# Context part of a gated delta kernel: silu ahead of a weight chunk's split, row sums from a repeated rate column

## The chip, the cores and the metric

One Trainium2 chip, one of its NeuronCores. The metric is device time in microseconds of one execution. Engines: PE (TensorE) multiplies, DVE (VectorE), ACT (ScalarE) and POOL (GpSimd) work elementwise, SP issues the weight loads.

## The reference, cut to what matters

Two model blocks over 256 positions of width 1024: a first block of two layers (attention, pooling, a feed-forward part of width 4096, a gate), and a second block whose mixer runs a chunked gated delta rule over a context and then over the latent positions. The change touches the inputs of that rule:

```python
qkv = jax.nn.silu(conv_fn(p_qkv, conv_w))        # then q, k, v; k is l2-normalized
g = -jnp.exp(a_log) * jax.nn.softplus(alpha + dt_bias)
g = jnp.cumsum(g, axis=-1)                       # per chunk, head and direction
decay = jnp.exp(jnp.where(lower, g[..., :, None] - g[..., None, :], -jnp.inf))
a = jnp.where(strict, jnp.einsum("bhnid,bhnjd->bhnij", kb, k) * decay, 0.0)
```

The kernel takes chunks of 128, two of them, four heads, two directions: four groups g = 0 to 3 of [128, 4 x 128]. The decay needs the cumulative sum of g once down the partitions and once along the row, the same row in all partitions: the row sums.

## The kernel before, in words

All values are fp32. A weight matrix comes in chunks of 1 MB from SP's queue into a ring of four raw slots. For the large projections each chunk is split in two halves into a high part (ACT, `split_hi`, line 534) and a low part (DVE, `split_lo`, line 543), in a ring of four pieces, and PE makes three products for each tile (lines 552 to 554). PE frees a piece when it has used it; a raw slot is free when its low parts are made.

The engines run programs in written order and meet at semaphores. PE's results go to eight PSUM banks. `Banks.claim` makes PE wait until all earlier uses of a bank are freed by their readers. In layer 1 the projections, the context's convolution inputs and the whole context delta part take banks 4 to 7 in turn (`ring([4, 5, 6, 7])`), in this order of claims: six query and key projections, `u`, three value projections, the context's rates, `ctx_c0` to `ctx_c3`, `out0`, two sums of squares `l20` and `l21`, `cum`, `out1`, `out2`, `kt0`, `vt0`, `kt1`, `vt1`, `out3`, and then the row sums `grow` and products `kk` with feed-forward steps between.

The context's delta part (`pe_delta`, `act_delta`, `dve_delta`, `pool_delta`, called with "ctx") runs in layer 1 between steps of the layer's own output projection and feed-forward part: `fill(point)` runs the next step, at all engines at the same point. Step `out0` (chunk 10) is at the point "ba", `out1` and `out2` (chunks 11 and 12) at "norm", `out3` at "tok", `up0` and on at "T0", "T1" ... The same functions run once more for the latent part.

Ahead of the delta part: the last convolution of the context's keys and values (ACT's middle line 749, DVE's sides lines 758 and 763); then ACT splits chunk 11 and makes the silu of keys and values in one instruction (line 1954), loads the table of logarithm and exponential (line 548), and begins `act_delta` with the exponentials and the logarithm of the rates (lines 988 to 991). DVE makes the low split of chunk 11, then the rates (lines 1114 to 1122), the squares of the keys (line 1132), the finished rates (lines 1136 to 1140, `dn_g`), and in the step of `out0` adds its bank to `h` (line 2467), which frees the bank. PE runs `out0`, sums the squares over the partitions with a matrix of ones (line 818), makes the cumulative sums (lines 825, 826), then `out1`. POOL waits for `dn_g`, makes four products of the triangular mask (`cum0` or `cum1`) with the rate columns of four heads (line 1297, `dn_tg`), then two copies of identity parts (line 1301). PE's row sum of a group is one matmul of ones with such a product (line 844).

Of the kernel before, what the change touches and what calls it, by code (L numbers as in the profile page):

```python
# [23 lines left out]
ALU = mybir.AluOpType  # L24
ACT = mybir.ActivationFunctionType
AX = mybir.AxisListType

P = 128
# [13 lines left out]
DN_H = 4  # L42
# [105 lines left out]
def vec_columns():  # L148
# [5 lines left out]
    for name, n in TILE_B:  # L154
# [25 lines left out]
LAST_FILL = 6 + len(LAT_FILL)  # L180


CTX_TOLD = dict(ba=1, ba2=1, sq=2, kn=2, rs=2, g=1, gcol=1, ecol=1, bcol=1, tok=1, tg=4,
                dl=4, el=4, A=4, P=2, T=2, XI=2, X=2 * LEVELS, Z=2 * (LEVELS - 1), N=2 * (LEVELS - 1), T2=2 * (LEVELS - 2),
                vb=4, kd=4, uw=4, vnew=2, state=4)

# [66 lines left out]
CTX_LAYER = 1  # L253
# [79 lines left out]
def two_blocks(nc, a, out):  # L333
    K, NK = const_columns()
    V, ROWS_A, NV = vec_columns()
    with ExitStack() as ctx:
# [5 lines left out]
        def S(name):  # L342
            if name not in sems:
                sems[name] = ctx.enter_context(nc.semaphore(name))
            return sems[name]
# [29 lines left out]
        ps = [ctx.enter_context(nc.psum_tensor(f"bank{b}", [P, 512], F32)) for b in range(8)]  # L375
# [23 lines left out]
        def col(name, i=0, n=1):  # L399
            s = K[name][0] + i  # L400
            return kt[:, s:s + n]
# [17 lines left out]
        g_X = A(4, 512)  # L419
# [96 lines left out]
        def chunk(layer, s):  # L516

            if s < LAYER_CHUNKS:
                return layer, s
            return (layer + 1, s - LAYER_CHUNKS) if layer + 1 < DEPTH else ("post", s - LAYER_CHUNKS)  # L520

        def split_hi(act, name, halves=(0, 1)):

            n = st.width(name)
            for half in halves:
                slot = st.piece(name, half)
                if name == (0, 0) and half == 0:
                    act.wait_ge(S("first_half"), 16)
                elif name == (0, 0) or half == 0:
                    act.wait_ge(landed[st.slot(name)], st.loads(name))  # L530
                v = st.pieces(name, half) - PIECES
                if v > 0:
                    act.wait_ge(pieces_done, v)
                nc.scalar.activation(whi[:, slot, 0:n], raw[:, st.slot(name), n * half:n * (half + 1)],  # L534
                                     ACT.Copy).then_inc(hi_ready, 1)
# [10 lines left out]
        def ln_exp_tables():  # L546

            nc.scalar.preload_act_table_set("natural_log_exp_and_others")
# [115 lines left out]
        def per_head(v):  # L664

            return v.unsqueeze(2).broadcast_to([P, DN_H, P])

        def all_heads(v):
            return v.unsqueeze(1).broadcast_to([P, DN_H, v.shape[1]])

        def h4(v):
            return v.rearrange("p (h n) -> p h n", h=DN_H)
# [5 lines left out]
        def chunk_of(g):  # L678
            return g // 2, g % 2
# [126 lines left out]
        def pe_delta(pe, part, d_, take, fill):  # L806
# [3 lines left out]
            F = banks.filled  # L810
# [18 lines left out]
            for n in range(TT):  # L829
                pe.wait_ge(*told("kn", 2))  # L830
                b = C(f"kt{n}")
                for hh in range(DN_H):
                    mm = nc.tensor.transpose(ps[b][:, P * hh:P * (hh + 1)], k_n[:, hh, P * n:P * (n + 1)], ident)
                F(mm, b)
                b = C(f"vt{n}")
                for hh in range(DN_H):
                    mm = nc.tensor.transpose(ps[b][:, P * hh:P * (hh + 1)], v_n[:, hh, P * n:P * (n + 1)], ident)
                F(mm, b)
            fill("tok")
            for i, g in enumerate(BY_CHUNK):  # L840
                d, n = chunk_of(g)
                pe.wait_ge(*told("tg", g + 1))
                b = C(f"grow{g}")
                F(nc.tensor.matmul(ps[b][:, :], ones, g_X[:, g, :], start=True, stop=True), b)
                if d == 0:
                    b = C(f"kk{g}")
                    for hh in range(DN_H):
                        kk = k_n[:, hh, P * n:P * (n + 1)]
                        mm = nc.tensor.matmul(ps[b][:, P * hh:P * (hh + 1)], kk, kk, start=True, stop=True)
                    F(mm, b)  # L850
                if lat and d == 0:
                    b = C(f"qk{g}")
                    if g == 0:
                        pe.wait_ge(S("lat_qn"), 2)
                    for hh in range(DN_H):
                        mm = nc.tensor.matmul(ps[b][:, P * hh:P * (hh + 1)], k_n[:, hh, P * n:P * (n + 1)],
                                              q_n[:, hh, P * n:P * (n + 1)], start=True, stop=True)
                    F(mm, b)
                fill(f"T{i}")
# [115 lines left out]
        def act_delta(act, part, d_, fill, settle=None):  # L975
# [13 lines left out]
            nc.scalar.activation(ba_t2, ba_t2, ACT.Exp, scale=-1.0)  # L989
            act.drain()  # L990
            nc.scalar.activation(ba_t2, ba_t2, ACT.Ln, bias=1.0).then_inc(S("dn_ba2"), 1)

            fill("ba")
            for i in range(4 if lat else 2):
# [102 lines left out]
        def dve_delta(dve, part, d_, fill):  # L1097
# [26 lines left out]

            nq = 4 if lat else 2
            first = 0 if lat else 4
            dve.wait_ge(S("silu"), 1 + len(lat_tiles) if lat else 1)
            for i in range(nq):
                v = sil[:, first + 2 * i:first + 2 * i + 2, :]
                if i >= 2:  # L1130
# [8 lines left out]
            nc.vector.reciprocal(ba_beta, ba_t1)  # L1139
            nc.vector.tensor_tensor(ba_g, ba_g, two(neg_a[:, :]), ALU.mult)  # L1140
            dve.drain().then_inc(S("dn_g"), 1)
            fill("ba")
            for i in range(nq):
                v = sil[:, first + 2 * i:first + 2 * i + 2, :]
# [143 lines left out]
        def pool_delta(pool, part, d_):  # L1288
            lat = part == "lat"
            told = lambda name, n: (S("dn_" + name), n + (CTX_TOLD[name] if lat else 0))  # L1290
            g_v = nc.gpsimd
            g_A, g_X, g_T = d_.A, d_.X, d_.T
            pool.wait_ge(*told("g", 1))
            for g in range(4):
                d, n = chunk_of(g)

                g_v.tensor_tensor(h4(g_X[:, g, :]), all_heads(col(f"cum{d}", 0, P)),
                                  per_head(d_.ba_g[:, n, 4 * d:4 * d + 4]), ALU.mult).then_inc(S("dn_tg"), 1)

            for n in range(TT):  # L1300
                g_v.tensor_copy(d_.rest(g_T, n), per_pair(ident))
            for n in range(TT if lat else 0):
                pool.wait_ge(*told("A", 2 * n + 2))
                g_v.tensor_tensor(g_A[:, n, :], g_A[:, n, :], g_A[:, 2 + n, :], ALU.add)
                pool.drain()
                g_v.tensor_tensor(h4(g_A[:, 2 + n, :]), h4(g_A[:, n, :]), all_heads(col("sib", 0, P)), ALU.mult)
                pool.drain().then_inc(S("dn_P"), 1)
                g_v.tensor_tensor(d_.other(g_T, n), per_pair(ident),
                                  g_A[:, 2 + n, :].rearrange("p (h n s) -> p h n s", h=DN_H, s=2), ALU.subtract)
                pool.drain().then_inc(S("dn_T"), 1)  # L1310
            if not lat:
                pool.drain().then_inc(S("ctx_rest"), 1)
                return
            pool.wait_ge(*told("ecol", 1))
            pool.wait_ge(*told("tok", 1))
            pool.wait_ge(S("lat_qn"), 2)
            for g in range(4):
                d, n = chunk_of(g)
                pool.wait_ge(S("lat_egrow"), BY_CHUNK.index(g) + 1)
                g_v.tensor_tensor(h4(g_q[:, g, :]), tok(d_.q, n), h4(g_q[:, g, :]), ALU.mult).then_inc(  # L1320
                    S("lat_qg"), 1)
            pool.wait_ge(S("lat_attn"), 4)
            pool.drain()
            for g in range(4):
                d, n = chunk_of(g)
                g_v.tensor_tensor(h4(d_.kd[:, g, :]), d_.ktok[:, n], per_head(d_.kd_col[:, g, :]), ALU.mult).then_inc(
                    S("dn_kd"), 1)
            pool.wait_ge(*told("bcol", 1))
            for g in range(4):
                d, n = chunk_of(g)  # L1330
                if g >= 2:
                    pool.wait_ge(*told("uw", g - 1))
                g_v.tensor_tensor(h4(d_.vb[:, g % 2, :]), d_.vtok[:, n], per_head(d_.beta_of(g)), ALU.mult)
                g_v.tensor_tensor(h4(d_.kb[:, g % 2, :]), d_.ktok[:, n], per_head(d_.bg_col[:, g, :]), ALU.mult)
                pool.drain().then_inc(S("dn_vb"), 1)
# [423 lines left out]
        def _(act):  # L1759
# [43 lines left out]
            for layer in range(DEPTH):  # L1803
# [122 lines left out]
                for kind, x in ATT[layer]:  # L1926
# [19 lines left out]
                    elif kind == "conv":  # L1946
                        act.wait_ge(direct_done, st.direct["ctx", x] + 1)
                        b = banks.bank(f"ctx_c{x}")
                        conv_middle(D_CTX.sil, b, 4 + 2 * x).then_inc(S("conv1"), 1)
                split_hi(act, chunk(layer, 11))  # L1950
                if layer == CTX_LAYER:
                    act.wait_ge(S("conv"), 4)
                    kv = D_CTX.sil[:, 4:12, :]
                    nc.scalar.activation(kv, kv, ACT.Silu).then_inc(S("silu"), 1)
                    ln_exp_tables()

                todo = list(range(10, 46))

# [228 lines left out]
        def _(dve):  # L2187
# [92 lines left out]
            for layer in range(DEPTH):  # L2280
# [166 lines left out]
                        free(ins, b)  # L2447
                    dve.drain().then_inc(S("cat_act"), 1)
                dve.drain().then_inc(S("side_free"), 1)
                split_lo(dve, chunk(layer, 11))  # L2450

                todo = list(range(10, 46))

# [403 lines left out]
```

## Time and profile before

| | us |
|---|---|
| median of 3 runs | 1300.92 (1298.52 to 1301.8) |
| the profiled execution's own time | 1299.26 |
| its span in the profile | 1297.5 |
| PE busy | 1248.8 |
| DVE busy | 872.7 |
| ACT busy | 640.3 |
| POOL busy | 93.5 |

An engine's busy time counts its instructions, not its waits. A matmul of unsplit fp32 operands leaves two records, and records of PE overlap, so times on PE are read from start to start. A row of a timeline merges consecutive instructions of one kind (xN); the bracket holds the idle time of the engine ahead of it and what ended it.

### The profile page before, as it was taken

To read this page: it belongs to the slowest core of one execution; us is meant where nothing else is said; L and a number is where in the kernel's file an instruction comes from. 1 tells how busy PE (TensorE), PEld (TensorE's weight loads), DVE (VectorE), ACT (ScalarE), POOL (GpSimd) and SP (SyncE) were. 2 spreads that over 40 slices of the span, in tenths; PEclk is the share of its full clock that TensorE was granted. 3 is DMA by queue.
4 is the path that set the end of the run, shared out by engine and by line. 5 is a ranking of instruction groups with operands and counts; after the bars stand their busy time and mean duration, and the time that the engine had idled before them with its cause. 6 is when DMAs were issued, how large, how long until landed. Compare 5 with 4: busy or idle time off the path is not lost.

```text
span 1297.5 us, 20646 instructions
## 1 busy us (share of the span) xinstructions
PE 1248.8 (96%) x8322; PEld 1107.1 (85%) x8322; DVE 872.7 (67%) x1312; ACT 640.3 (49%) x974; POOL 93.5 (7%) x84
## 2 busy tenths in 40 slices
PE   7989999999999998999999999999899999999997
PEld 7979778888998887899999889986789988888886
DVE  6886656667778478765646776785467776766665
ACT  6574434335656364545364665552254555444443
POOL 0330000000024020000000000324100000000000
PEclk9999999999999999999999999999999999999999
DMA  9634776555663453544543665537115556555530
GB/s 329 196 100 163 265 256 225 194 179 189 224 210 100 133 160 98 163 131 134 175 142 105 197 191 145 181 98 250 43 53 175 194 183 235 199 194 195 189 136 33
DMA packets 164620, 219.35 MB, mean 169 GB/s; under 512 B 5456, under 2 KB 135342, under 8 KB 164398
## 3 DMA queue, kind: packets, MB, share of 16 engines
q1 hardware_dynamic: 162800, 214.45, 50.9%
q10 hardware_dynamic: 1726, 3.59, 0.7%
q8 instruction: 66, 1.08, 0.4%
q14 instruction: 28, 0.23, 0.1%
HBM read 216.19 MB, written 1.05 MB: 167 GB/s over the span
## 4 chain that ended last, share of the span: by engine, by line
PE 75%; DVE 12%; ACT 4%; DVEq 3%; issue 2%; DMA 2%; SPq 1%; ACTq 1%
PE bank L552 14%; PE bank L596 14%; PE bank L554 13%; PE bank L553 13%; PE bank L598 7%; DVE w_lo L543 4%; PE bank L642 2%; DMA arena<-arena 2%; PE bank L886 1%; PE bank L874 1%; ACT w_hi L534 1%; PE bank L1438 1%; PE bank L1417 1%; SPq L2811 1%; PE bank L903 1%
## 5 line engine op out<-in xcount | busy, mean ns | idle before, releaser
L543 DVE TENSOR_TENSOR w_lo<-w_raw,w_hi 128x1024 fp32r<-128x1024 f32 (+1 forms) x350 | 418.0, 1239 | 86.1 <-ACT w_hi L534 78.4
L534 ACT ACTIVATE w_hi<-w_raw 128x1024 fp32r<-128x1024 f32 (+1 forms) x350 | 347.0, 1039 | 93.0 <-PE bank L554 58.1
L596 PE MATMUL bank<-act_parts,w_hi 128*128 128x512 f32 x800 | 283.7, 398 | 2.8 <-DVE act_parts L2206 1.4
L552 PE MATMUL bank<-act_parts,w_hi 128*128 128x256 f32 x944 | 272.1, 288 | 10.3 <-DVE w_lo L543 5.2
L554 PE MATMUL bank<-act_parts,w_lo 128*128 128x256 f32 x944 | 267.7, 284 | 0.0
L553 PE MATMUL bank<-act_parts,w_hi 128*128 128x256 f32 x944 | 267.7, 284 | 0.0
L598 PE MATMUL bank<-act_parts,w_lo 128*128 128x256 f32 x800 | 224.0, 280 | 0.0
L552 PEld LDWEIGHTS bank<-act_parts,w_hi 128*128 128x128 f32 x944 | 181.6, 192 | 19.0 <-issue 13.5
L596 PEld LDWEIGHTS bank<-act_parts,w_hi 128*128 128x128 f32 x800 | 150.1, 188 | 45.0 <-issue 7.2
L553 PEld LDWEIGHTS bank<-act_parts,w_hi 128*128 128x128 f32 x944 | 181.7, 193 | 0.5 <-issue 0.5
L554 PEld LDWEIGHTS bank<-act_parts,w_lo 128*128 128x128 f32 x944 | 181.6, 192 | 0.0
L552 PE MATMUL bank<-w_hi,side_hi 128*128 128x512 f32 (+1 forms) x392 | 150.1, 383 | 1.5 <-DVE w_lo L543 1.5
L598 PEld LDWEIGHTS bank<-act_parts,w_lo 128*128 128x128 f32 x800 | 151.0, 189 | 0.3
L554 PE MATMUL bank<-w_hi,side_lo 128*128 128x512 f32 (+1 forms) x392 | 148.0, 378 | 0.0
L553 PE MATMUL bank<-w_lo,side_hi 128*128 128x512 f32 (+1 forms) x392 | 147.7, 377 | 0.0
L608 DVE TENSOR_REDUCE arena<-bank 128x256 f32<-128x512 f32 x100 | 64.4, 686 | 84.9 <-PE bank L598 84.9
L552 PEld LDWEIGHTS bank<-w_hi,side_hi 128*128 128x128 f32 x392 | 73.8, 188 | 20.0 <-issue 6.8
L554 PEld LDWEIGHTS bank<-w_hi,side_lo 128*128 128x128 f32 x392 | 73.7, 188 | 14.0
L553 PEld LDWEIGHTS bank<-w_lo,side_hi 128*128 128x128 f32 x392 | 73.8, 188 | 12.3
L1980 ACT ACTIVATE side_hi<-arena 128x512 fp32r<-128x512 f32 x32 | 20.2, 632 | 118.6 <-DVE arena L2483 103.4
L552 PE MATMUL bank<-side_hi,w_hi 128*128 128x256 f32 x208 | 60.4, 291 | 4.5 <-DVE w_lo L543 4.5
L553 PE MATMUL bank<-side_lo,w_hi 128*128 128x256 f32 x208 | 59.6, 287 | 0.0
(333 smaller groups left out, 1606.4 us busy)
## 6 DMA issues: line engine op xcount, KB each, us to landing
w_raw<-in_w_in SPq DMA_DIRECT2D x39, 1024.0 KB, 6.0
w_raw<-in_w_up SPq DMA_DIRECT2D x32, 1024.0 KB, 5.6
w_raw<-in_w_down SPq DMA_DIRECT2D x32, 1024.0 KB, 5.0
w_raw<-in_w_mod SPq DMA_DIRECT2D x24, 1024.0 KB, 5.4
w_raw<-in_w_ffn_in SPq DMA_DIRECT2D x22, 1024.0 KB, 5.2
w_raw<-in_w_gate SPq DMA_DIRECT2D x20, 1024.0 KB, 5.1
w_raw<-in_w_ffn_out SPq DMA_DIRECT2D x11, 1024.0 KB, 5.4
w_raw<-in_w_out SPq DMA_DIRECT2D x8, 1024.0 KB, 5.1
```

The costliest lines, as they stand in the source:

```text
L534: nc.scalar.activation(whi[:, slot, 0:n], raw[:, st.slot(name), n * half:n * (half + 1)], ACT.Copy).then_inc(hi_ready, 1)
L543: nc.vector.tensor_tensor(wlo[:, slot, 0:n], raw[:, st.slot(name), n * half:n * (half + 1)], whi[:, slot, 0:n].bitcast(F32), ALU.subtract) ...
L552: nc.tensor.matmul(o, ahi, bhi, start=start, stop=False, skip_group_check=True)
L553: nc.tensor.matmul(o, ahi, blo, start=False, stop=False, skip_group_check=True)
L554: return nc.tensor.matmul(o, alo, bhi, start=False, stop=stop, skip_group_check=True)
L596: nc.tensor.matmul(pair(two_banks[m]), whi[:, slot, at:at + P], xall[:, :, f, :], start=f == 0, stop=False, skip_group_check=True)
L598: mm = nc.tensor.matmul(o[:, 0:T], wlo[:, slot, at:at + P], xhi[:, f, :], start=False, stop=f == KT - 1, skip_group_check=True)
L608: return nc.vector.tensor_reduce(to, ps[b][:, :].rearrange("p (s t) -> p t s", s=2), AX.X, ALU.add)
L642: mm = nc.tensor.matmul(ps[bank][:, T * m:T * (m + 1)], raw[:, st.slot(name), at:at + P], act[:, k, :], start=k == 0, stop=k == KT - 1)
L874: mm = nc.tensor.matmul(ps[b][:, P * hh:P * (hh + 1)], h4(g_A[:, n, :])[:, hh, :], d_.x_new_of(n, hh, lv), start=True, stop=True)
L886: mm = nc.tensor.matmul(ps[b][:, P * hh:P * (hh + 1)], h4(z_sm[:, n, :])[:, hh, :], d_.t_new_of(n, hh, lv), start=True, stop=True)
L1980: nc.scalar.activation(yhi[:, 2 * (j % 2):2 * (j % 2) + 2, :], relu2[j % 2], ACT.Copy).then_inc(S("relu_hi"), 1)
```

## The change

For the context, the split of chunk 11 moves from ahead of the silu (ACT) and ahead of the rates (DVE) to behind the rates' logarithm (ACT) and behind the finished rates (DVE), in both cases still ahead of the step of `out0`. The silu of keys and values becomes two instructions, keys first; DVE's squares wait for the first alone, PE's transposes of values for the second. Layer 0 keeps its order. In both parts, context and latent, POOL's four products are gone; each row sum is four matmuls, one for each head, whose weights are the head's rate column repeated in 128 columns and whose moving operand is the mask itself.

```diff
--- before.py
+++ after.py
@@ -180,7 +180,7 @@
 LAST_FILL = 6 + len(LAT_FILL)
 
 
-CTX_TOLD = dict(ba=1, ba2=1, sq=2, kn=2, rs=2, g=1, gcol=1, ecol=1, bcol=1, tok=1, tg=4,
+CTX_TOLD = dict(ba=1, ba2=1, sq=2, kn=2, rs=2, g=1, gcol=1, ecol=1, bcol=1, tok=1,
                 dl=4, el=4, A=4, P=2, T=2, XI=2, X=2 * LEVELS, Z=2 * (LEVELS - 1), N=2 * (LEVELS - 1), T2=2 * (LEVELS - 2),
                 vb=4, kd=4, uw=4, vnew=2, state=4)
 
@@ -833,15 +833,19 @@
                     mm = nc.tensor.transpose(ps[b][:, P * hh:P * (hh + 1)], k_n[:, hh, P * n:P * (n + 1)], ident)
                 F(mm, b)
                 b = C(f"vt{n}")
+                if not lat:
+                    pe.wait_ge(S("silu"), 2)
                 for hh in range(DN_H):
                     mm = nc.tensor.transpose(ps[b][:, P * hh:P * (hh + 1)], v_n[:, hh, P * n:P * (n + 1)], ident)
                 F(mm, b)
             fill("tok")
             for i, g in enumerate(BY_CHUNK):
                 d, n = chunk_of(g)
-                pe.wait_ge(*told("tg", g + 1))
                 b = C(f"grow{g}")
-                F(nc.tensor.matmul(ps[b][:, :], ones, g_X[:, g, :], start=True, stop=True), b)
+                for hh in range(DN_H):
+                    rate = d_.ba_g[:, n, 4 * d + hh:4 * d + hh + 1].broadcast_to([P, P])
+                    mm = nc.tensor.matmul(ps[b][:, P * hh:P * (hh + 1)], rate, col(f"cum{d}", 0, P), start=True, stop=True)
+                F(mm, b)
                 if d == 0:
                     b = C(f"kk{g}")
                     for hh in range(DN_H):
@@ -989,6 +993,8 @@
             nc.scalar.activation(ba_t2, ba_t2, ACT.Exp, scale=-1.0)
             act.drain()
             nc.scalar.activation(ba_t2, ba_t2, ACT.Ln, bias=1.0).then_inc(S("dn_ba2"), 1)
+            if not lat:
+                split_hi(act, chunk(CTX_LAYER, 11))
 
             fill("ba")
             for i in range(4 if lat else 2):
@@ -1124,7 +1130,7 @@
 
             nq = 4 if lat else 2
             first = 0 if lat else 4
-            dve.wait_ge(S("silu"), 1 + len(lat_tiles) if lat else 1)
+            dve.wait_ge(S("silu"), 2 + len(lat_tiles) if lat else 1)
             for i in range(nq):
                 v = sil[:, first + 2 * i:first + 2 * i + 2, :]
                 if i >= 2:
@@ -1139,6 +1145,8 @@
             nc.vector.reciprocal(ba_beta, ba_t1)
             nc.vector.tensor_tensor(ba_g, ba_g, two(neg_a[:, :]), ALU.mult)
             dve.drain().then_inc(S("dn_g"), 1)
+            if not lat:
+                split_lo(dve, chunk(CTX_LAYER, 11))
             fill("ba")
             for i in range(nq):
                 v = sil[:, first + 2 * i:first + 2 * i + 2, :]
@@ -1291,12 +1299,6 @@
             g_v = nc.gpsimd
             g_A, g_X, g_T = d_.A, d_.X, d_.T
             pool.wait_ge(*told("g", 1))
-            for g in range(4):
-                d, n = chunk_of(g)
-
-                g_v.tensor_tensor(h4(g_X[:, g, :]), all_heads(col(f"cum{d}", 0, P)),
-                                  per_head(d_.ba_g[:, n, 4 * d:4 * d + 4]), ALU.mult).then_inc(S("dn_tg"), 1)
-
             for n in range(TT):
                 g_v.tensor_copy(d_.rest(g_T, n), per_pair(ident))
             for n in range(TT if lat else 0):
@@ -1947,12 +1949,14 @@
                         act.wait_ge(direct_done, st.direct["ctx", x] + 1)
                         b = banks.bank(f"ctx_c{x}")
                         conv_middle(D_CTX.sil, b, 4 + 2 * x).then_inc(S("conv1"), 1)
-                split_hi(act, chunk(layer, 11))
                 if layer == CTX_LAYER:
-                    act.wait_ge(S("conv"), 4)
-                    kv = D_CTX.sil[:, 4:12, :]
-                    nc.scalar.activation(kv, kv, ACT.Silu).then_inc(S("silu"), 1)
+                    for half in range(2):
+                        act.wait_ge(S("conv"), 2 * half + 2)
+                        part = D_CTX.sil[:, 4 + 4 * half:8 + 4 * half, :]
+                        nc.scalar.activation(part, part, ACT.Silu).then_inc(S("silu"), 1)
                     ln_exp_tables()
+                else:
+                    split_hi(act, chunk(layer, 11))
 
                 todo = list(range(10, 46))
 
@@ -2447,7 +2451,8 @@
                         free(ins, b)
                     dve.drain().then_inc(S("cat_act"), 1)
                 dve.drain().then_inc(S("side_free"), 1)
-                split_lo(dve, chunk(layer, 11))
+                if layer != CTX_LAYER:
+                    split_lo(dve, chunk(layer, 11))
 
                 todo = list(range(10, 46))
```

## Rows read from the trace of the kernel before

**Rows 1.** The page's part 1: busy time, share of the span, instructions.
```profile
PE 1248.8 (96%) x8322; PEld 1107.1 (85%) x8322; DVE 872.7 (67%) x1312; ACT 640.3 (49%) x974; POOL 93.5 (7%) x84
```

**Rows 2.** Chain of waits, 453 to 466 us: start us, us, what.
```profile
460.98 0.70 DVE arena L1132
461.73 1.98 PE bank L818 x4
```

**Rows 3.** Timeline of PE, 459 to 468: start, us, operation, [idle before, releaser].
```profile
459.97 0.28 PE L554 MATMUL bank<-act_parts,w_lo 128*128 128x256 f32 x1
461.73 1.98 PE L818 MATMUL bank<-arena,consts_sb 128*128 128x512 f32 x4 [1.48 <-DVE arena L1132]
463.55 0.28 PE L825 MATMUL bank<-arena,consts_sb 128*128 128x4 f32 x2
465.25 0.36 PE L552 MATMUL bank<-act_parts,w_hi 128*128 128x256 f32 x1
```

**Rows 4.** Timeline of DVE there.
```profile
457.37 2.36 DVE L543 TENSOR_TENSOR w_lo<-w_raw,w_hi 128x1024 fp32r<-128x1024 f32 x2 [0.23 <-ACT w_hi L534]
459.65 0.22 DVE L1114 TENSOR_REDUCE arena<-bank 128x16 f32<-128x64 f32 x1
463.08 0.69 DVE L2467 TENSOR_TENSOR h<-h,bank 128x512 f32<-128x512 f32 x1
466.57 4.01 DVE L543 TENSOR_TENSOR w_lo<-w_raw,w_hi 128x1024 fp32r<-128x1024 f32 x2
```

**Rows 5.** Timeline of ACT there.
```profile
454.45 0.83 ACT L749 ACTIVATE arena<-bank,vec_cols 128x256 f32<-128x256 f32 x2
455.16 2.01 ACT L534 ACTIVATE w_hi<-w_raw 128x1024 fp32r<-128x1024 f32 x2
458.49 1.92 ACT L1954 ACTIVATE arena<-arena 128x2048 f32<-128x2048 f32 x1
460.42 1.28 ACT L548 ACT_TABLE_LOAD   x1
462.23 1.99 ACT L534 ACTIVATE w_hi<-w_raw 128x1024 fp32r<-128x1024 f32 x2
```

**Rows 6.** Timeline of PE, behind the fourth context row sums.
```profile
511.31 0.35 PE L552 MATMUL bank<-act_parts,w_hi 128*128 128x256 f32 x1 [3.45 <-DVE w_lo L543]
```

**Rows 7.** Timeline of PE, the transposes of values.
```profile
478.18 0.66 PE L837 MATMUL bank<-consts_sb,arena 128*128 128x128 f32 x4 [0.73 <-DVE arena L1153]
```

**Rows 8.** Timeline of POOL: context products and copies, latent products.
```profile
463.07 4.49 POOL L1297 TENSOR_TENSOR arena<-consts_sb,arena 128x512 f32<-128x512 f32 x4 [50.07 <-DVEq L1141]
467.50 4.08 POOL L1301 COPY arena<-consts_sb 128x512 f32<-128x512 f32 x2
...
815.70 6.46 POOL L1297 TENSOR_TENSOR arena<-consts_sb,arena 128x512 f32<-128x512 f32 x4 [344.12 <-DVEq L1141]
```

**Rows 9.** Timeline of SP and of ACT: a load's issue, its first reader.
```profile
459.76 0.37 SPq L2795 DMA_DIRECT2D w_raw<-in_w_up  x1
...
490.16 1.04 ACT L534 ACTIVATE w_hi<-w_raw 128x1024 fp32r<-128x1024 f32 x1
```

**Rows 10.** Chain of waits: row sums, key products; line 844's weight loads.
```profile
842.83 0.86 PE bank L844 x2
843.69 0.89 PE bank L849 x8
...
L844 PEld LDWEIGHTS bank<-arena,consts_sb x16: 188/191/192, 485.4 to 866.1; 128*128 128x128 f32 x16
```

**Rows 11.** What PE waited for, 796 to 880: total us, times, longest.
```profile
PE bank L866 <- POOLq L1307: 1.2, 1, 1.2
PE bank L552 <- DVE w_lo L543: 1.0, 1, 1.0
```

**Rows 12.** Stretches: window, length, busy of PE, PEld, DVE, ACT, POOL, PEclk, DMA.
```profile
461.70:465.20 3.50, 3.47 (x20) 2.52 (x20) 1.79 (x6) 3.33 (x8) 2.13 (x3) 1.00 0.81 265
511.98:515.36 3.38, 3.38 (x19) 3.38 (x17) 2.51 (x7) 1.63 (x3) 0.00 (x0) 0.50 0.53 131
```

## The prediction

> **What bounds the kernel now.** I read the page first: TensorE is busy 96% of the span, DVE 67%, ACT 49%, POOL 7% [rows 1]. So an edit on DVE, ACT or POOL is worth only the TensorE idle time that it removes or makes. Then the chain of waits around the place of the edit, and the timelines of the engines there.
>
> The chain shows how the context stage starts. TensorE finishes `out0` (last record from 459.97), has nothing, and starts the sums of squares at 461.73: 1.48 us idle, released by the DVE square of line 1132 [rows 2, 3]. On DVE that square stands behind the low split of weight chunk 11 (457.37 to 459.73) and the small rate operations (from 459.65) [rows 2, 4]. On ACT the high split of chunk 11 (455.16 to 457.17) stands ahead of the table load, the silu of keys and values, the second table load and the rates' exponentials [rows 5]. The edit takes both splits out of the way. The later stalls of this stage (3.45 us before 511.31, behind a low split) hang on DVE work that starts from `out3`, hence from TensorE, and move along with it [rows 6].
>
> **ACT and DVE, as they will run.** ACT, from the end of the last conv middle (454.45 + 0.83 = 455.28): table load 1.28, silu of keys, silu of values. The two halves have 128x1024 elements each. The trace has no silu of that size; the whole took 1.92, and a pair of 128x1024 copies 2.01, so I take 2.0 for the pair and 1.06 for the first. The second half waits for conv 4, which DVE ends at 457.14, before the first half ends at 457.6. So silu 1 is up at 457.65, silu 2 at 458.6, the second table load ends at 459.9, where it ended at 461.70: everything behind it is 1.8 us earlier [rows 5]. DVE has the rates from 457.3 instead of 459.65, ends them after the same 1.33 (460.98 minus 459.65), and squares at 458.6 and 459.2; the first square is written by 459.3. TensorE is then still in `out0`, so its 1.48 us are gone, and counted from record to record (461.73 minus 459.97 + 0.12) 1.6 us. The rates' logarithm comes 1.8 earlier, the finished rates at 463.05 - 1.8 = 461.25. TensorE wants them when the sums of squares are issued (1.82 after their start in the trace, so 462.0): no wait. The eight pairs of cumulative sums take 463.55 to 465.25, 1.70; they end at 463.7 [rows 3].
>
> **What is late next.** After them comes `out1`. It needs chunk 11, whose splits now stand behind the rates. ACT: 1.8 earlier than the split at 462.23, so 460.4 to 462.4 [rows 5]. DVE: from 461.5, and `out1` could read the first half at 462.7 to 463.5. That is early enough. But `out1` also claims a bank. The part takes banks 4 to 7 in turn; in the order of claims `out0` is number 16, the two sums of squares 17 and 18, the cumulative sums 19, `out1` number 20. So `out1` has the bank of `out0`, and waits until DVE has added `out0` to `h` (line 2467). I trust this count because it says the same of the transposes of values: they would have the bank of the cumulative sums, and the trace shows just that wait, 0.73 us on the copy of line 1153 [rows 7]. Before, the residual ran at 463.08 to 463.77, straight after the rates, and TensorE came at 465.25: 1.5 us of slack. Now the split of chunk 11 stands between the rates and the residual on DVE.
>
> How long is that split? Alone the two halves take 2.36 (457.37), while POOL works 4.01 (466.57) [rows 4]. POOL no longer makes its four products, 4.49 us; its two copies, 4.08 us, follow the rates at once, at 461.25 to 465.3, where they ran from 467.50 [rows 8]. In the trace these very copies lay beside the low split of chunk 12 and made it 4.01. So the removed products don't free DVE here, they bring the copies forward onto chunk 11. The low end is 2.36: the split ends at 463.9, the residual (0.69) at 464.55, and `out1` starts 0.7 earlier than before. The high end is 4.01: split to 465.5, residual to 466.1, `out1` at 466.15, against 465.25: 0.9 later. I take the high end, because both engines and both operations are the same as they were at 466.57 [rows 4, 8].
>
> The Trainium skill (SBUF — State Buffer, "SBUF: two separate sides") says that of a VectorE operation with two inputs in SBUF and a GpSimd operation that reads SBUF the one that starts second waits for the whole of the first. Estimated by that rule, with 1.12 for a copy alone (a quarter of POOL's four products), the split would start at 462.4, wait once more between its halves, and end at 465.9 instead of 465.5, and `out1` start 1.3 later instead of 0.9. The trace agrees that they collide (4.01 against 2.36), and the durations from it stand in my sum.
>
> TensorE is then idle from 463.7 to 466.15, some 2.4 us in place of 1.48. Behind it: the normalized keys (ACT's reciprocal root at about 465.6, 0.1 later than before) follow the residual on DVE at 466.1, the split of chunk 12 follows without POOL beside it (2.36, to 469.2), and `out2` wants it after 5.8 us of `out1`, at 471.9: no further wait. SP's load that needs chunk 11 split is issued some 5.7 us later than at 459.76; its data is first read at 490.16, by ACT: hidden [rows 9]. The load behind it needs chunk 12's split, which ends at 469.2 instead of 470.6. The transposes of values wait for silu 2, long there.
>
> **Row sums.** Each of eight becomes four fp32 matmuls of 128 columns in place of one of 512. Of the new kind the nearest is the keys' product: 8 records 0.89, the old 2 records 0.86: +0.03 each, 0.24 for eight [rows 10]. The weights are one column repeated, whose load I bound from both sides: nothing more than a full tile (0.89), or its load (191 ns) eight times in a row, 1.52, +0.66 each. I take the first, since the keys' products have eight such loads too and don't show them. Of the eight, those of the context lie ahead of the 3.45 us stall, which swallows them. Of the latent ones I count 0.1 in all. The latent part's POOL products (6.46 us) go too; nobody waited for them: between 796 and 880 TensorE waits 1.2 on POOL's parts after the decays and 1.0 on a weight split, neither of them behind the products [rows 8, 11]. DVE gets faster beside a shorter POOL there, at no gain on TensorE: 0.
>
> **Sum.** -1.6 for the stall, +2.5 for the new wait on the bank (net +0.9 at `out1`), +0.1 for the row sums: +1.0 us. The profiled execution took 1299.26 (span 1297.5 and 1.76 around it), so 1300.3; the median of the runs shown lies 1.66 above that execution, so 1301.9 against 1300.92. A change below 0.3%, 3.9 us, can't be told from none here.
>
> **Rivals.**
> (a) The copies and the split don't collide, or POOL's copies are through sooner: the low end above, -0.7 + 0.1 = -0.6, so 1300.3. For it: spans on POOL are rough, and the first copy starts a moment before the split. Against it: both copies together last longer than a lone split.
> (b) No wait on the bank at all: the full -1.6 + 0.1, 1299.4. Against it stand the count and the wait in [rows 7].
> (c) Slower: the longer idle time drops the clock. After the 3.45 us stall the trace shows TensorE at 0.50 of its clock (1.2 GHz) for 3.38 us, so 1.7 us of work lost; after the 1.48 us stall it stays at 1.00 [rows 3, 6, 12]. The new gap of 2.4 lies between. There the loss was covered by DVE; in `out1` nothing covers it: +1.0 + 1.7 = +2.7, 1303.6. It decides if a gap of 2.4 us is already enough, and it costs all that was won at the sums of squares, and more. The Trainium skill (TensorE: Matmul & The Clock Gate, "The HAM clock gate") says that idleness throttles the engine to half clock; by it this case is possible and not sure.
> (d) Slower: the repeated column is dear, the high end above. Context mostly covered by the stall, latent four at +0.66, and two of the context that the stall does not cover: +4.0 on top of +0.9, 1305.8.
>
> **How the numbers follow.** Forecast 0.50, (a) 0.17, (b) 0.08, (c) 0.18, (d) 0.03, other 0.04. The runs shown differ by 3.3 us among themselves, so a median is uncertain by more than these cases differ. Range 1298.0 to 1305.0. Faster by over 0.3% (below 1297.0) would take (b) and luck: 0.03; slower by over 0.3% (above 1304.8) takes (d), or (c) and bad luck: 0.05; within: 0.92.
>
> **What would show it.** In the profile after: the sums of squares start within 0.2 us of `out0`'s end; then a TensorE idle of 2 to 2.6 us before `out1`, released by line 2467's residual; the low split of chunk 11 just ahead of that at about 2 us a half, with POOL's copies beside it from 461.3; no POOL products. Halves at 1.2 mean (a); no idle ahead of `out1` means that the bank count is wrong, (b); half clock in `out1` means (c); row sums of more than 0.9 us mean (d).

## The result, and the profile after

| | before | after |
|---|---|---|
| median | 1300.59 us (1298.28 to 1302.26, 20 runs) | 1302.57 us (1300.61 to 1305.89, 20 runs) |
| ratio | | 1.0021, 95% interval 1.0014 to 1.0027 |
| profiled execution's span | 1297.5 | 1302.3 |

The changed kernel is 0.2% slower, 2.7 us by the ratio. That is inside the range and below the 0.3% that were set as a bound, but its interval is clear of 1. The likeliest case had +1.0; +2.7 is what rival (c), half clock in `out1`, was priced at.

The page's part 1 of the changed kernel, against [rows 1]: TensorE works 2.9 us longer, POOL 12.5 less.

```profile
PE 1251.7 (96%) x8370; PEld 1113.9 (86%) x8370; DVE 869.0 (67%) x1312; ACT 640.3 (49%) x975; POOL 81.0 (6%) x76
```

The timeline of TensorE at the same place, against [rows 3]. `out0`'s end to the sums of squares: no idle any more. The cumulative sums end at 463.7; then TensorE idles 2.16 us, and what ends it is line 2472, DVE's residual of `out0`:

```profile
460.20 1.88 PE L818 MATMUL bank<-arena,consts_sb 128*128 128x512 f32 x4
461.91 0.28 PE L825 MATMUL bank<-arena,consts_sb 128*128 128x4 f32 x2
465.92 0.58 PE L552 MATMUL bank<-act_parts,w_hi 128*128 128x256 f32 x1 [2.16 <-DVE h L2472]
```

The timeline of DVE, against [rows 4]. The rates come first, then the squares; the low split of chunk 11 takes 3.66 us in place of 2.36, and the residual waits behind it. Chunk 12's split, 4.01 before, takes 2.35:

```profile
457.47 0.23 DVE L1120 TENSOR_REDUCE arena<-bank 128x16 f32<-128x64 f32 x1 [0.23 <-issue]
458.81 1.29 DVE L1138 TENSOR_TENSOR arena<-arena 128x512 f32<-128x512 f32 x2
461.61 3.66 DVE L543 TENSOR_TENSOR w_lo<-w_raw,w_hi 128x1024 fp32r<-128x1024 f32 x2 [0.34 <-ACT w_hi L534]
465.19 0.67 DVE L2472 TENSOR_TENSOR h<-h,bank 128x512 f32<-128x512 f32 x1
466.61 2.35 DVE L543 TENSOR_TENSOR w_lo<-w_raw,w_hi 128x1024 fp32r<-128x1024 f32 x2
```

ACT, against [rows 5]: the two halves of the silu (x2, 2.01), the table load, and one run of four high splits (chunks 11 and 12). POOL, against [rows 8]: only the copies are left, beside chunk 11's low split, in 3.00 us where they took 4.08.

```profile
455.40 1.28 ACT L1956 ACT_TABLE_LOAD   x1
456.70 2.01 ACT L1956 ACTIVATE arena<-arena 128x1024 f32<-128x1024 f32 x2
458.72 1.28 ACT L548 ACT_TABLE_LOAD   x1
460.53 3.88 ACT L534 ACTIVATE w_hi<-w_raw 128x1024 fp32r<-128x1024 f32 x4
```

```profile
461.36 3.00 POOL L1303 COPY arena<-consts_sb 128x512 f32<-128x512 f32 x2 [48.26 <-DVEq L1147]
```

Four stretches of the changed kernel, with columns as in [rows 12] (window, length, busy of PE, PEld, DVE, ACT, POOL, granted clock, DMA). In the 7 us from the start of `out1` TensorE is busy all the time at a mean clock of 0.57: 3.0 us of work lost. Ahead of the gap it had 1.00, and the clock fell inside the gap: it is 1.00 up to 464.76 and 0.50 from 465.26 on. After the first stall of the stage, 3.35 us long, it stays at 1.00 (514.65 to 519.90). It has half clock once more, for about 3.4 us, after the second stall:

```profile
458.00:464.00 6.00, 5.76 (x40) 4.71 (x38) 4.76 (x12) 5.90 (x9) 2.64 (x2) 1.00 0.01 1
465.92:472.92 7.00, 7.00 (x36) 7.00 (x37) 2.96 (x3) 1.06 (x1) 0.00 (x0) 0.57 0.86 281
514.65:519.90 5.25, 5.25 (x44) 5.25 (x45) 4.17 (x9) 2.53 (x3) 0.00 (x0) 1.00 0.58 161
523.20:526.20 3.00, 3.00 (x7) 2.43 (x8) 2.30 (x4) 1.38 (x2) 0.00 (x0) 0.50 0.32 33
```

The two stalls of DVE's stretch in the changed kernel; [rows 6] has the first of them:

```profile
514.65 0.36 PE L552 MATMUL bank<-act_parts,w_hi 128*128 128x256 f32 x1 [3.35 <-DVE w_lo L543]
523.20 0.77 PE L552 MATMUL bank<-w_hi,side_hi 128*128 128x512 f32 x1 [2.56 <-DVE w_lo L543]
```

Starts of the same matmuls in both traces show where the 4.8 us of the two profiled executions come from: `out1` 465.25 and 465.92 (+0.67); first matmul after the stall of 3.4 us, 511.31 and 514.65 (+3.34); second stall 519.91 and 523.20 (+3.29); the first matmul of the step after that, 526.59 and 531.12 (+4.53); the last transposes 1290.02 and 1294.95 (+4.93). So +0.7 is the wait, +2.7 the half clock in `out1`, and +1.2 the second half clock, behind the second stall; the last 0.4 arises later in the kernel, and its cause is open. The trace before has half clock in this stage only after the first stall (from 511.98), where DVE is the bound. Where half clock falls behind the two stalls is a matter of the single execution, and so is the +1.2: the medians differ by 2.0.

A row sum and a product of keys in the latent part, in the chain of waits, against [rows 10]: 0.89 each.

```profile
847.32 0.89 PE bank L847 x8
848.21 0.89 PE bank L853 x8
```

### The profile page after: what moved, and what is told of

The parts are those of the page before. It is cut to its first block, busy times and chain, and to the rows that moved or that the text cites. A ratio compares the mean times of both kernels' runs of the same rounds, so it can differ in the third digit from the quotient of the medians.

```text
span 1302.3 us, 20729 instructions
## 1 busy us (share of the span) xinstructions
PE 1251.7 (96%) x8370; PEld 1113.9 (86%) x8370; DVE 869.0 (67%) x1312; ACT 640.3 (49%) x975; POOL 81.0 (6%) x76
## 4 chain that ended last, share of the span: by engine, by line
PE 77%; DVE 11%; ACT 5%; DVEq 3%; issue 2%; DMA 2%; ACTq 1%; SPq 0%
PE bank L552 14%; PE bank L554 14%; PE bank L553 14%; PE bank L596 14%; PE bank L598 7%; DVE w_lo L543 4%; PE bank L642 2%; PE bank L890 1%; PE bank L1419 1%; PE bank L878 1%; PE bank L1440 1%; DMA arena<-arena 1%; ACT w_hi L534 1%; PE bank L907 1%; DVE arena L1239 1%
## 5 line engine op out<-in xcount | busy, mean ns | idle before, releaser
L554 PE MATMUL bank<-side_hi,w_lo 128*128 128x256 f32 x208 | 59.6, 286 | 0.0
```

The lines of the kernel that those rows point to most:

```text
L554: return nc.tensor.matmul(o, alo, bhi, start=False, stop=stop, skip_group_check=True)
```

## The experiments

All ratios are against the kernel before, on the same chip, 95% interval in brackets. Executions differ by up to 3.3 us in when they reach this place, so `out1` is told from the start of the last convolution middle on ACT (line 749), which lies ahead of all that is changed. In the trace before that distance is 465.25 - 454.45 = 10.80 us. "Clock" is the mean granted clock in the 7 us from the start of `out1`. "At the stall" measures from the same ACT instruction to the first matmul after the stage's first stall, the one at 511.31 in the trace before (distance 56.86), and gives the difference to before: what a kernel has lost or won when `out1` and the steps behind it are done. Gap, distances and clock come from the one profiled execution of each kernel, the ratio from all its executions.

| kernel | gap before `out1` | distance | against before | clock | at the stall | ratio |
|---|---|---|---|---|---|---|
| before | none | 10.80 | | 1.00 | | |
| changed | 2.16 | 11.37 | +0.57 | 0.57 | +3.24 | 1.0021 (1.0014 to 1.0027) |
| e1 matmuls in the gap | 0.17 | 11.39 | +0.59 | 1.00 | +0.61 | 1.0002 (0.9993 to 1.0011) |
| e2 `out1` in another bank | none | 9.06 | -1.74 | 1.00 | -1.72 | 0.9987 (0.9978 to 0.9996) |
| e3 residual first | none | 9.06 | -1.74 | 1.00 | -1.73 | 0.9985 (0.9977 to 0.9994) |
| e4 copies late | 0.86 | 10.07 | -0.73 | 0.77 | +0.72 | 1.0002 (0.9994 to 1.0011) |
| e5 order only | 2.37 | 11.58 | +0.78 | 0.59 | +3.32 | 1.0033 (1.0023 to 1.0044) |
| e6 row sums only | none | 10.80 | 0.00 | 1.00 | +0.01 | 1.0001 (0.9992 to 1.0009) |
| e7 residual first, products kept | none | 9.09 | -1.71 | 1.00 | -1.72 | 0.9990 (0.9982 to 0.9999) |
| e8 changed, again | 2.15 | 11.35 | +0.55 | 0.62 | +2.92 | 1.0026 (1.0017 to 1.0035) |
| e9 residual first, silu whole | 0.28 | 10.90 | +0.10 | 1.00 | +0.11 | 0.9999 (0.9991 to 1.0008) |

Where the clock is 1.00, the two differences agree within 0.02 us. Where it is not, the second is larger, by 2.67 in the changed kernel, 1.45 in e4, 2.54 in e5 and 2.37 in e8: that is what the half clock costs by position.

The theory from the two traces: the wait on the bank costs 0.6 us and the clock the rest. The rivals: `out1` is late by its weights; the new row sums are dear; the clock has nothing to do with the gap.

**e1, matmuls in the gap.** On the changed kernel, 16 matmuls of 256 columns whose results nobody reads:

```diff
             F(mm, b)
+            if not lat:
+                pe.wait_ge(banks.free[0], banks.n_use[0])
+                for i in range(16):
+                    nc.tensor.matmul(ps[0][:, 0:T], xhi[:, 0, 0:P], xhi[:, 1, :], start=True, stop=True)
             fill("norm")
```

> The changed kernel, with 16 matmuls of 256 columns added on TensorE between the cumulative sums and out1, in the context part. They write a bank that nobody reads then, and take some 1.9 of the 2.16 us in which TensorE waits for the bank of out0. Nothing else is changed. Theory (the wait on the bank delays out1 by 0.7 us, and the rest of the loss is half clock after the gap, in out1 and once more behind it): out1 still starts 0.6 to 0.8 us later than in the kernel before, the clock stays at 1.00 from 464 to 480, and the time is 0.7 to 1.0 us above the kernel before (ratio 1.0005 to 1.0008) instead of 2.7 above. Rival (the clock has nothing to do with the gap, or the loss is in DVE's or POOL's order): half clock in out1 as in the changed kernel, ratio 1.002.

PE's timeline and the 7 us from `out1`: the added matmuls fill the gap, `out1` starts no earlier than in the changed kernel, and its clock is 1.00.

```profile
463.47 2.15 PE L831 MATMUL bank<-act_parts 128*128 128x256 f32 x16
465.79 0.38 PE L552 MATMUL bank<-act_parts,w_hi 128*128 128x256 f32 x1 [0.17 <-DVE h L2476]
465.79:472.79 7.00, 7.00 (x58) 7.00 (x59) 3.65 (x4) 2.02 (x2) 0.00 (x0) 1.00 0.92 279
```

With useless work put into the gap the time falls from 1.0021 to 1.0002 (1.0005 to 1.0008 was expected; the interval covers that), though `out1` starts as late as in the changed kernel: the clock's loss hangs on the gap. Of the loss of 2.7 us, 2 to 2.5 are the clock: 2.5 by the two ratios (give or take some 1.4, from their intervals), 2.1 if the 0.6 of the wait is taken off, and 2.67 in the profiled execution. The mean granted clock of a whole execution points the same way: 0.9917 to 0.9923 in the three kernels with a gap above 2 us (changed, e5, e8), 0.9933 to 0.9950 in all others. It can't be turned into time, since it counts idle stretches too: e2 has the lowest of the others, 0.9933, and is among the fastest, and its trace has half clock through the last 6.7 us, in which TensorE is busy for 2.6.

**e2, another bank.** `out1` takes a bank of the lower four, and the ring of the upper four is stepped once all the same, so that every other use keeps its bank:

```diff
                     if kind == "out":
-                        b = C(f"out{j}")
+                        if layer == CTX_LAYER and j == 1:
+                            high()
+                            b = CL(f"out{j}")
+                        else:
+                            b = C(f"out{j}")
```

> The changed kernel, with out1 in a bank of the lower four (the upper ring is still stepped once, so every other use has the bank that it had). Theory (out1 waits for nothing but the bank of out0): the gap of 2.16 us before out1 closes to below 0.2 us, out1 starts about 1.5 us earlier than in the kernel before, no half clock there, and the time is 1.4 us below the kernel before (ratio 0.9989, between 0.998 and 0.9995). Rival (out1 waits for its weights, whose low split stands behind the rates): the gap stays, at least 1.5 us of it, released by the low split, and the ratio stays at 1.002.

PE goes from the cumulative sums to `out1` without a wait, while DVE's residual of `out0` ends 2.3 us later:

```profile
464.12 0.36 PE L826 MATMUL bank<-arena,consts_sb 128*128 128x4 f32 x2
464.34 0.36 PE L552 MATMUL bank<-act_parts,w_hi 128*128 128x256 f32 x1
...
465.95 0.67 DVE L2476 TENSOR_TENSOR h<-h,bank 128x512 f32<-128x512 f32 x1
```

The bank is the wait; the weights are in time. Ratio 0.9987, as expected (0.9989).

**e3, the residual first.**

```diff
-            if not lat:
-                split_lo(dve, chunk(CTX_LAYER, 11))
             fill("ba")
+            if not lat:
+                split_lo(dve, chunk(CTX_LAYER, 11))
```

> The changed kernel, with DVE's residual of out0 ahead of its low split of chunk 11 instead of behind it. Theory: the residual runs at 461.4 to 462.1 and frees the bank in time; the low split follows at 462.1 beside POOL's copies, its first half ends at 463.7 to 464.1, so that out1 starts at 463.8 to 464.2, 1.1 to 1.5 us earlier than in the kernel before; no half clock; ratio 0.999 (0.998 to 0.9997). Rival (the weights are as late as the bank): out1 starts at 465 or later, ratio 1.000 or above.

DVE's timeline and PE's start of `out1`. The low split begins 0.8 us after the residual did, and PE starts `out1` at 462.58 without waiting:

```profile
460.35 0.69 DVE L2472 TENSOR_TENSOR h<-h,bank 128x512 f32<-128x512 f32 x1
461.17 3.12 DVE L543 TENSOR_TENSOR w_lo<-w_raw,w_hi 128x1024 fp32r<-128x1024 f32 x2
...
462.58 0.36 PE L552 MATMUL bank<-act_parts,w_hi 128*128 128x256 f32 x1
```

This kernel beats the one before (0.9985; 1298.61 against 1300.31 us) and the changed one (1.0021). The expectation had `out1` 1.1 to 1.5 us earlier, it was 1.74: the split took 3.12 us, less than with the copies fully beside it. The residual, which reads a bank, took 0.69 beside a copy, against 0.68 in e4 without one.

**e4, the copies later.**

```diff
+            if not lat:
+                pool.wait_ge(*told("tok", 1))
             for n in range(TT):
                 g_v.tensor_copy(d_.rest(g_T, n), per_pair(ident))
```

> The changed kernel, with POOL's two copies for the context held back until ACT has copied keys and values (line of dn_tok, some 20 us later, where their result is not yet wanted). Theory (the copies lengthen the low split of chunk 11, 3.66 instead of 2.36 us): the split takes 2.36 us, out1 starts at 464.6 to 464.8, 0.6 us earlier than in the kernel before, after a gap of 0.9 us; no half clock; ratio 0.9995 (0.999 to 1.000). Rival (the split is slow for another reason, as ACT's high split beside it): the split still takes over 3.3 us, ratio 1.002.

```profile
461.85 2.36 DVE L543 TENSOR_TENSOR w_lo<-w_raw,w_hi 128x1024 fp32r<-128x1024 f32 x2 [0.34 <-ACT w_hi L534]
...
464.87 0.58 PE L552 MATMUL bank<-act_parts,w_hi 128*128 128x256 f32 x1 [0.86 <-DVE h L2474]
...
464.87:471.87 7.00, 7.00 (x46) 7.00 (x47) 2.96 (x3) 2.06 (x3) 0.00 (x0) 0.77 0.72 217
```

The low split alone takes 2.36, as ever, so its length was POOL's doing. `out1` starts 0.73 earlier than before (0.6 expected). But TensorE has half clock again, at a gap of only 0.86 us: 3.4 us of it, and at the stall the kernel is 0.72 late where it was 0.73 early. The ratio is 1.0002. The expectation "no half clock" was wrong.

The trace before has a gap of 1.48 us at 461.73 with 1.00 after it [rows 3, 12]: the length of the gap alone does not tell. Two readings are open. One: it depends on what lies ahead, before 5.8 us of `out0`, here the sums of squares and the cumulative sums with 4 columns each (which alone, without a gap, leave the clock at 1.00 in e2, e3 and e7). The other: it differs from one execution to the next, whatever lies ahead. For that speaks the first stall of the stage in two executions of one program: its 3.35 us are followed by half clock from about 515.3 on in e8, and by 1.00 in the changed kernel's trace. No run varied the work ahead by itself, and only one execution of e4 was profiled, so neither is shown.

**e5, the order alone**, and **e6, the row sums alone**: the kernel before with one half of the change each (the parts of the diff for `dn_tg`, line 844 and line 1297 in e6, all others in e5).

> The order of splits and silu as changed, the row sums as in the kernel before (POOL's products kept, one matmul for each row sum). Theory (the loss is from the order alone; POOL's products lengthen chunk 11's low split just as its copies do, and the copies then lie beside chunk 12's): low split of chunk 11 at 3.7 to 4.1 us, a gap of 2.2 to 2.7 us before out1, out1 0.7 to 1.2 us later than in the kernel before, half clock there, ratio 1.002 (1.001 to 1.003). Rival (the loss comes from the new row sums or from POOL's copies moving forward alone): ratio 1.000 or below, gap under 1.5 us.

> The row sums as changed, the order of splits and silu as in the kernel before. Theory (row sums are worth nothing either way): out1 starts as in the kernel before (within 0.1 us), each row sum takes 0.89 us in place of 0.86, ratio 1.0001 (0.9995 to 1.0007). Rival (they carry part of the loss by their weights, 0.66 us each on TensorE): row sums above 1.2 us, ratio 1.002 or more.

e5: POOL's products lie beside chunk 11's low split and make it 3.87 us, and the gap is 2.37.

```profile
463.63 6.45 POOL L1303 TENSOR_TENSOR arena<-consts_sb,arena 128x512 f32<-128x512 f32 x4 [48.27 <-DVEq L1145]
470.03 4.00 POOL L1307 COPY arena<-consts_sb 128x512 f32<-128x512 f32 x2
...
463.87 3.87 DVE L543 TENSOR_TENSOR w_lo<-w_raw,w_hi 128x1024 fp32r<-128x1024 f32 x2 [0.34 <-ACT w_hi L534]
...
468.39 0.58 PE L552 MATMUL bank<-act_parts,w_hi 128*128 128x256 f32 x1 [2.37 <-DVE h L2476]
```

e6: POOL's copies run at once after the rates, alone in 2.07 us, and are over before chunk 12's split, which takes 2.35 in place of 4.01; the 1.47 us ahead of the sums of squares stay.

```profile
464.13 2.07 POOL L1297 COPY arena<-consts_sb 128x512 f32<-128x512 f32 x2 [50.05 <-DVEq L1143]
...
467.23 2.35 DVE L543 TENSOR_TENSOR w_lo<-w_raw,w_hi 128x1024 fp32r<-128x1024 f32 x2
...
462.81 0.70 PE L818 MATMUL bank<-arena,consts_sb 128*128 128x512 f32 x1 [1.47 <-DVE arena L1134]
```

The loss is the order's alone; the expectations of both held, but for e5's ratio, expected at 1.002 (1.001 to 1.003) and found at 1.0033. The row sums are worth nothing by themselves (1.0001, 0.9992 to 1.0009). Beside the copies alone the low split is a little shorter (3.66 against 3.87), and `out1` 0.2 us less late; the ratios, 1.0021 and 1.0026 against 1.0033, have intervals that meet and don't show it.

**e7, residual first with the products kept** (e5 with e3's edit).

> The kernel with the residual of out0 ahead of the low split of chunk 11, but with the row sums as in the kernel before (POOL's products kept). Theory (once the bank is freed in time, the splits have slack enough, with or without products beside them): no gap before out1, ratio 0.9987 (0.998 to 0.9995), the same as with the new row sums. Rival (without the products' removal the low split of chunk 11, at 2 us a half, or kept company by POOL longer, is late for out1): a gap of 0.5 us or more before out1 or in its middle, ratio above 0.9995.

```profile
463.03 3.27 DVE L543 TENSOR_TENSOR w_lo<-w_raw,w_hi 128x1024 fp32r<-128x1024 f32 x2
...
462.20 6.46 POOL L1303 TENSOR_TENSOR arena<-consts_sb,arena 128x512 f32<-128x512 f32 x4 [48.27 <-DVEq L1145]
```

The split takes 3.27 us beside the products, and `out1` still does not wait. At the stall both are 1.72 to 1.73 ahead; whether the row sums add anything to e3 elsewhere stays open (0.9990 and 0.9985, wide intervals).

**e8, the changed kernel once more.**

> The changed kernel itself, on the same chip as the three others. Theory: the gap of 2.1 to 2.3 us before out1 in every execution; whether half clock follows and for how long (3.4 or 6.8 us in the profiles so far) may differ, so its times spread wider than those of a kernel without the gap; ratio 1.002 (1.001 to 1.003). Rival (the earlier measurement was by chance): ratio 1.0005 or less.

```profile
465.73 0.58 PE L552 MATMUL bank<-act_parts,w_hi 128*128 128x256 f32 x1 [2.15 <-DVE h L2472]
...
465.73:472.73 7.00, 7.00 (x39) 7.00 (x40) 2.96 (x3) 1.06 (x1) 0.00 (x0) 0.62 0.93 282
```

The loss is there again: 1.0026 (1.0017 to 1.0035). The twelve executions run from 1299.32 to 1306.10, 6.8 us, against 5.0 for the 34 of the kernel before beside them. The fastest had the highest mean clock of the twelve, 0.995, and the slowest the lowest, 0.989. So how much half clock an execution gets seems to differ; where it fell is known for the profiled one alone.

**e9, the silu whole** (e3 with one silu for keys and values, behind the fourth convolution).

> The kernel with the residual of out0 ahead of the low split of chunk 11, and the silu of keys and values again as one instruction, which waits for the fourth convolution. Theory (only the splits' move counts; the rates keep DVE until 458.7 anyway, and the whole silu ends at about 458.8): squares within 0.3 us of where they were, no gap before the sums of squares or out1, ratio 0.9986 (0.998 to 0.9995). Rival (the early silu of keys carries the gain): squares 1 us or more later, a new gap before the sums of squares, ratio 0.9993 or above.

ACT, DVE and PE:

```profile
457.46 1.28 ACT L1955 ACT_TABLE_LOAD   x1 [1.99 <-DVEq L2436]
...
460.70 1.29 DVE L1138 TENSOR_TENSOR arena<-arena 128x512 f32<-128x512 f32 x2 [1.92 <-ACT arena L1955]
...
461.45 1.12 PE L818 MATMUL bank<-arena,consts_sb 128*128 128x512 f32 x2 [1.01 <-DVE arena L1138]
465.54 0.36 PE L552 MATMUL bank<-act_parts,w_hi 128*128 128x256 f32 x1 [0.28 <-DVE w_lo L543]
```

The theory failed, the rival holds. The silu's table load (1.28 us) stands on ACT behind the silu's wait for the fourth convolution. With the halves it runs while DVE still makes that convolution (455.40 in the changed kernel); as one instruction it starts at 457.46, after 1.99 us idle, so the squares come 1.8 us later and TensorE waits 1.01 for them and 0.28 for the low split. The halves are what makes the move of the splits pay: `out1` comes 1.84 us later without them than in e3, and the ratio is 0.9999 against 0.9985 (intervals that just meet). The clock stayed at 1.00 here, behind gaps of 1.01 and 0.28 with the cumulative sums between them.

## Why the prediction was right, and where not

- **The stall of 1.48 us goes**: right. Squares expected at 458.6, found at 458.81; table loads' end 459.9 and 460.0; finished rates 461.25 and about 461.35.
- **A wait on the bank takes its place**: right, and e2 and e3 show it. `out1` was expected at 466.15, found at 465.92; a gap of 2.4, found 2.16. The term was +0.9 and measured +0.57 (the distance above) to +0.67.
- **The copies lengthen the low split**: right (e4); 4.01 expected, 3.66 found. Taken one by one, the two halves of the split and the two copies end in turn, at 462.48 (copy), 463.39 (half), 464.36 (copy) and 465.26 (half), each 0.9 to 1.0 us after the one before it:

```profile
461.36 1.12 POOL L1303 COPY arena<-consts_sb 128x512 f32<-128x512 f32 x1 [48.26 <-DVEq L1147]
461.61 1.78 DVE L543 TENSOR_TENSOR w_lo<-w_raw,w_hi 128x1024 fp32r<-128x1024 f32 x1 [0.34 <-ACT w_hi L534]
462.32 2.04 POOL L1303 COPY arena<-consts_sb 128x512 f32<-128x512 f32 x1
463.31 1.95 DVE L543 TENSOR_TENSOR w_lo<-w_raw,w_hi 128x1024 fp32r<-128x1024 f32 x1
```

The same order of ends in the trace before gives the 4.01 (467.55 product, then half, copy, half, copy at 468.63, 469.67, 470.58, 471.58): there a product ran on for 0.98 us after the split of chunk 12 had begun, here the first copy for 0.87. The prediction carried over the duration (4.01, and 4.08 for the copies, which took 3.00) and not the order. By the Trainium skill (SBUF — State Buffer, "SBUF: two separate sides") the one that starts second waits for the whole of the first; the prediction's estimate by it had the split end at 465.9, the trace has 465.27. The ends in turn agree with that page: each operation ends one operation's time after the other engine's. A recorded span that starts earlier than that seems to hold the wait (the second copy's 2.04 against some 1.0 alone, from 2.07 for two in e6); the estimate was 0.6 too late since it took 1.2 for each half, and behind a copy's end a half took 0.9.
- **Row sums +0.1**: the size of each was right (0.89); e6 has 1.0001 (0.9992 to 1.0009).
- **The clock**: this is the step that failed. The forecast let the clock stay at 1.00, a term of nothing, and gave half clock 0.18, since the trace of before had none after 1.48 us. All three profiles with a gap of 2.15 to 2.37 us (changed, e5, e8) show it, and e1 takes it away. Rival (c) put the sum at +2.7, which is what the ratio gives; part of that agreement is luck, as the wait was 0.3 smaller than forecast and the clock's share is 2 to 2.5. Its price of 1.7 came from the 3.38 us at half clock in [rows 12]; in the three profiles the half clock in the gap and `out1` lasts about twice that, and cost 2.4 to 2.7 by position.
- **Rivals (a), (b), (d)**: (a) fell with the split at 3.66, (b) with the gap, (d) with 0.89 a row sum.

The range and the chance of "within 0.3%" held. The likeliest case gave the sign and not the size: +1.0 forecast, +2.7 (1.8 to 3.5 by the interval) measured.

## What to carry to other kernels

When work is moved back on an engine to let something urgent pass, list what now stands behind it, and for each what it frees: here the loss was not at the weights that the moved split makes, but at a residual that frees a PSUM bank. Count the ring of banks to find who waits for whom, and check the count on a wait that the trace has already. A gap in TensorE costs its own length and, if half clock follows, more than that: 1.5 to 2.7 us in the four profiles that have it in `out1`. The length of a gap alone did not tell here whether half clock follows, so price both cases.

## What was not expected of the hardware

- Half clock came after a gap of 0.86 us behind small matmuls (e4), and did not come after 1.48 us behind large ones (before; 1.47 in e6), nor after a stall of 3.35 us in the changed kernel's own trace. Each is one execution, and what decides it is not shown.
- Sixteen useless matmuls, 2.15 us of work, made the changed kernel some 2.5 us faster (ratio 1.0002 against 1.0021).
- The table load of an activation came only after the wait written ahead of that activation: 1.28 us on the path in e9, hidden where the first activation's inputs are ready early.
- POOL's two copies take 2.07 us alone, 3.00 beside DVE's two subtractions, which take 3.66 in place of 2.36: the four end in turn. DVE's residual, with one input in a bank, is not lengthened beside a copy (0.69 in e3, 0.68 in e4 without).
